# Pairs of up projection tiles in parts 1 to 3 computed as seven block products of quarter sums

## The chip, the cores and the metric

The kernel runs on one core of a Trainium2 chip. The metric is the device time of one execution in microseconds (us). The profile is that of one execution, taken by the hardware profiler.

## The reference, cut to what matters

One inference step of a streaming encoder with two layers (`DEPTH = 2`). 512 prompt rows and 8 x 16 sample rows make 640 rows of 1024 features in float32. Each layer has two kinds of attention and then a feed-forward, which is all that the change touches:

```python
def finish_layer(x, a, b, ga, gb, w_a, w_b, w_o, g1, b1, w_up, w_down, g2, b2):
    mix = (ga * (a @ w_a) + gb * (b @ w_b)) @ w_o
    x = layer_norm(ALPHA * x + mix, g1, b1)
    h = jnp.square(jax.nn.relu(x @ w_up)) @ w_down      # w_up 1024 x 4096, w_down 4096 x 1024
    return layer_norm(ALPHA * x + h, g2, b2)
```

## The kernel before

**Numbers in two halves.** Every float32 operand of a product is split: ScalarE writes a rounded high half (type float32r), and VectorE the low half, value minus high. A product of two operands is three matmuls: high x high, high x low, low x high. `high` and `low` do this for a chunk of weights (128 partitions x 1024), `x_high` and `x_low` for the input, held transposed as `xt_hi` and `xt_lo`, 8 blocks of 128 features by 640 rows.

**The weights** are one stream of chunks of 512 KB. SP loads them in order into four slots of `raw`; the load of a chunk waits (`w_ready`) until the low half of the chunk four places before is made, which frees its slot. Two working slots `s` = 0 and 1 (`w_hi`, `w_lo`) are used in turn. Chunks are counted in pairs: `n` is the pair, `nth` gives it for a place in the stream. Some slots more (`LAST_ROWS`, `NEXT`) lie in the region `r_b`.

**The feed-forward** is cut into four parts of 1024 hidden features (`FF_PARTS`). A part has 8 up tiles (four pairs `u`, `s` = 0 and 1) and then two row groups of down products. `feature_tile` computes one up tile, 128 hidden features by 640 rows: two halves of 320 rows (`HALF`), each a bank of PSUM, 8 blocks `k` and three matmuls in each. Tile `s` uses the banks 4 + 2s and 5 + 2s (`pair(s)`). ScalarE takes the tile out by a ReLU into `tmp1`, makes the high half of the weights of the next pair, VectorE squares into `tmp2`, makes the low half of those weights, ScalarE copies the square's high half, and VectorE writes its low half. The hidden features go to `act_b` in parts 0 and 2 and to `act_a` in parts 1 and 3. `row_group` is a half of the down product: for each `k` and each of five row tiles `r`, three matmuls of 512 columns, into the banks 0, 1, 2, 3 and 7 (`ROW_BANKS`). VectorE adds each finished bank into `rows` (`take`).

**Order.** Each engine runs its own list in order and waits on semaphores (`wait_ge`), written out by hand. `chunk_half_done[s]` and `chunk_done[s]` count the halves of a chunk's matmuls that TensorE has finished, `w_ready[s]` the low halves of weights, `h_ready` the hidden tiles, `relu_done[s]` the tiles taken out of PSUM, `row_evacuated[r]` the row banks taken. Both engines handle the weights of the next pair while TensorE works on this one:

```python
for u in range(0, KT // 2):
    for s in range(2):
        t = l * 32 + part * 8 + 2 * u + s
        act.wait_ge(chunk_done[s], nth(l, AT_FF) + part * 8 + u + 1)
        act.wait_ge(sq_done, t)
        fn(halves(tmp1[:]), pair(s), ACT.Relu).then_inc(relu_done[s], 1)
        high(s, nth(l, AT_FF, 1) + part * 8 + u)
        wait_apart(act, sq_done, t + 1)
        fn(hidden[0][:, 2 * u + s, :], tmp2[:], ACT.Copy).then_inc(h_hi_ready, 1)
```

Of the kernel before, what the change touches and what calls it, by code (L numbers as in the profile page):

```python
# [18 lines left out]
F32 = mybir.dt.float32  # L19
# [20 lines left out]
HALF = ROWS // 2  # L40
BANK = 512
FF_PARTS = 4
ALPHA = (2 * DEPTH) ** 0.25
EPS = 1e-5
QK_SCALE = DH ** -0.5
# [41 lines left out]
def build(nc, x_rows, k_cache, v_cache, swa_kc, swa_vc, swa_k_keep, swa_v_keep, weights, cols,  # L87
# [3 lines left out]
    with ctx:  # L91
# [36 lines left out]
        for hi_at, lo_at in ((0, 4096), (20480, 24576), (8192, 28672), (12288, 16384), (32768, 36864)):  # L128
            n = len(w_hi)
            w_hi.append(at([r_b[0] + hi_at, r_b[1]], f"w_hi{n}", [D], F32R))  # L130
            w_lo.append(at([r_b[0] + lo_at, r_b[1]], f"w_lo{n}", [D], F32R))
        LAST_ROWS, NEXT = (2, 3, 0, 4), (5, 6)

        cos = at(r_keep, "cos", [ROWS], F32)
# [49 lines left out]
        d_rs = at(rb, "d_rs", [P], F32)  # L184
        rb = list(r_b)
        act_b = [at(rb, "act_b_hi", [KT, ROWS], F32R), at(rb, "act_b_lo", [KT, ROWS], F32R)]

        rm = list(r_mix)
        u_p = [at(rm, f"u_p{p}", [2, BANK], F32) for p in range(2)]
# [6 lines left out]
        rm = list(r_mix)  # L196
        ln_g = at(rm, "ln_g", [D], F32)
        ln_b = at(rm, "ln_b", [D], F32)
        rr = list(r_rows)
        s_p = at(rr, "s_p", [8, P], F32)  # L200
        s_pt = at(rr, "s_pt", [8, P], F32)
# [28 lines left out]

        def halves(t):
            return t.rearrange("p (a n) -> p a n", a=2)


        raw_loaded = [sem(f"raw_loaded{j}") for j in range(RAW_SLOTS)]
# [58 lines left out]
        input_rows, out_stored = sem("input_rows"), sem("out_stored")  # L294
        relu_done = [sem(f"relu_done{s}") for s in range(2)]
        sq_done, h_hi_ready, h_ready = sem("sq_done"), sem("h_hi_ready"), sem("h_ready")
        y_stored, keep_stored = sem("y_stored"), sem("keep_stored")
        newton = sem("newton")
        waits_passed = sem("waits_passed")
# [49 lines left out]
        def transposed_tile(r):  # L349

            bank = (4, 0, 2, 0, 2)[r]
            return PS[:, bank:bank + 2, :].rearrange("p a (k n) -> p (a k) n", n=P)

        def norm_tile(l, which, r):
            return (2 * l + which) * RT + r
# [70 lines left out]
        def _(pe):  # L426
            mm = nc.tensor.matmul

            def feature_tile(s, n, hi, lo, which, part=None, between=None, slot=None, order=None):
# [5 lines left out]
                for half, k in order:  # L435
# [8 lines left out]
                    if k == KT - 1:  # L444
                        last.then_inc((chunk_half_done if half == 0 else chunk_done)[s], 1)

            def row_group(n, group, hi, lo, before_k=None, between=None, before_bank=None, banks=ROW_BANKS):

                if between is not None:
# [5 lines left out]
                for k, r in steps:  # L455
                    s, k2 = (k // 2) % 2, k % 2
                    if r == 0:
                        if k2 == 0:
                            pe.wait_ge(w_ready[s], n + (k // 4 + 1))
                        if before_k:  # L460
                            before_k(k)
                    slot = LAST_ROWS[k // 2] if between is not None else s
                    if between and (r, k) in between:
                        between[r, k]()
                    wh = w_hi[slot][:, k2 * BANK:(k2 + 1) * BANK]
                    wl = w_lo[slot][:, k2 * BANK:(k2 + 1) * BANK]
                    if k == 0:

                        pe.wait_ge(row_evacuated[r], group)
                        if r == RT - 1 and before_bank:  # L470
                            before_bank()
# [317 lines left out]
            for l in range(DEPTH):  # L789
# [2 lines left out]

                for v in range(0, 2):
                    row_group(nth(l, AT_V) + 2 * v, l * GROUPS + v, xt_hi, xt_lo,
                              before_bank=lambda: rope_pair_free(l * ROPES + 1), banks=V_BANKS)

                all_heads(pe, l, head)
                last_head_end(l)
# [80 lines left out]
                for v in range(2):  # L879
# [4 lines left out]
                              before_bank=lambda: pe.wait_ge(branch_taken, l * 16 + 16))  # L884

                for part in range(FF_PARTS):
                    hidden = act_b if part % 2 == 0 else act_a
                    if part == 0:

                        first_tiles(l, 1, nth(l, AT_FF))  # L890
                    for u in range(1 if part == 0 else 0, KT // 2):
                        for s in range(2):

                            pe.wait_ge(relu_done[s], l * 16 + 4 * part + u)
                            if s == 1:

                                pe.wait_ge(row_evacuated[RT - 1], l * GROUPS + 4 + 2 * part)
                            feature_tile(s, nth(l, AT_FF) + 8 * part + u, xt_hi, xt_lo, s)
                    def down(v, between=None):
                        row_group(nth(l, AT_FF) + 8 * part + 4 + 2 * v, l * GROUPS + 4 + 2 * part + v,  # L900
                                  hidden[0], hidden[1],
                                  lambda k: pe.wait_ge(h_ready, l * 32 + 8 * part + k + 1), between,

                                  lambda: pe.wait_ge(relu_done[1], l * 16 + 4 * part + 4))

                    if part < FF_PARTS - 1:
                        for v in range(0, 2):
# [7 lines left out]
        def _(act):  # L915
# [310 lines left out]
            def normalise(l, which):  # L1226
# [13 lines left out]
                if more:  # L1240
                    x_high(*at_x, 3)
                    x_high(*at_x, 4)

            eps = col[:, C_EPS:C_EPS + 1]
            act.preload_act_table_set("natural_log_exp_and_others")
            high(0, 0, NEXT[0])
# [8 lines left out]
            for l in range(DEPTH):  # L1255
# [65 lines left out]
                last_groups_high(nth(l, AT_O), True)  # L1321
                normalise(l, 0)

                act.wait_ge(ln_rows, RT * (l + 1))
                load_norm(l, 1)
                for part in range(FF_PARTS):
                    hidden = act_b if part % 2 == 0 else act_a
                    for u in range(0, KT // 2):
                        for s in range(2):
                            t = l * 32 + part * 8 + 2 * u + s  # L1330
                            act.wait_ge(chunk_done[s], nth(l, AT_FF) + part * 8 + u + 1)
                            act.wait_ge(sq_done, t)
                            fn(halves(tmp1[:]), pair(s), ACT.Relu).then_inc(relu_done[s], 1)  # L1333
                            high(s, nth(l, AT_FF, 1) + part * 8 + u)
                            wait_apart(act, sq_done, t + 1)
                            fn(hidden[0][:, 2 * u + s, :], tmp2[:], ACT.Copy).then_inc(h_hi_ready, 1)

                    down = nth(l, AT_FF, 4) + part * 8
                    if part < FF_PARTS - 1:
                        group_high(down)  # L1340
                        for i in (3, 4):
                            for s in range(2):
                                high(s, down + i)
# [11 lines left out]
        def _(dve):  # L1355
# [377 lines left out]
            def half_rows(h):  # L1733
                return lambda r: rows[:, r, bass.ts(h, BANK)]


            v.memset(mask_cols[:], 0.0).then_inc(masks_ready, 1)
            low(0, 0, NEXT[0])
# [31 lines left out]
            for l in range(DEPTH):  # L1770
# [41 lines left out]
                wait_apart(dve, x_rows_loaded, 16 * (l + 1))  # L1812
                take_last_but_one(l * GROUPS + 2, nth(l, AT_O), ALPHA, True)
                take_and_normalise(l, 0, l * GROUPS + 3, nth(l, AT_O) + 2, ALPHA)
                for part in range(FF_PARTS):
                    hidden = act_b if part % 2 == 0 else act_a
                    for u in range(0, KT // 2):
                        for s in range(2):
                            t = l * 32 + part * 8 + 2 * u + s
                            dve.wait_ge(relu_done[s], l * 16 + part * 4 + u + 1)  # L1820
                            dve.wait_ge(h_ready, t)
                            v.tensor_tensor(tmp2[:], tmp1[:], tmp1[:], ALU.mult).then_inc(sq_done, 1)  # L1822
                            low(s, nth(l, AT_FF, 1) + part * 8 + u)
                            dve.wait_ge(h_hi_ready, t + 1)
                            v.tensor_tensor(hidden[1][:, 2 * u + s, :], tmp2[:],
                                            hidden[0][:, 2 * u + s, :].bitcast(F32), ALU.subtract)\
                                .then_inc(h_ready, 1)


                    wait_apart(dve, ln_rows, RT * (l + 1))  # L1830
                    group, n = l * GROUPS + 4 + 2 * part, nth(l, AT_FF) + 8 * part + 4
                    if part < FF_PARTS - 1:
                        for half in range(0, 2):
                            take_group(group + half, n + 2 + 2 * half, half, ALPHA if part == 0 else 1.0)
# [157 lines left out]
```

## Time and profile before

| | |
|---|---|
| Runs | 2302.49, 2303.79, 2306.5 us; median 2303.79 |
| The profiled execution: its own time, its span | 2303.64 us, 2301.8 us |
| TensorE busy | 2257.1 us, 98% of the span |
| VectorE busy | 1129.2 us, 49% |
| ScalarE busy | 914.0 us, 40% |
| Mean granted clock of TensorE | 0.996 of full speed |
| DMA | 107 GB/s over the span |

The span is from the first to the last instruction; a run's own time holds a little around it. Engines are named PE (TensorE matmul), PEld (TensorE weight load), DVE (VectorE), ACT (ScalarE), SP (SyncE, which issues the weight loads). L441 is line 441 of the kernel. Lines of helpers stand for all that they record: L441 to L443 are the matmuls of every feature tile, L474 to L476 those of every row group, L926 every high half of weights, L1396 every low half. Matmuls are pipelined, so each is shown longer than the step from one to the next.

### The profile page before, as it was taken

The numbers are of one execution on the slowest core, as the hardware profiler recorded it, in microseconds if no ns is written. First come the engines' busy times: TensorE is split into PE (matmuls) and PEld (weight loads), VectorE is DVE, ScalarE is ACT, GpSimd is POOL, SyncE is SP. The second block draws the span as 40 slices with busy tenths as digits, with TensorE's granted clock in tenths as the row PEclk, the third lists the DMA queues.
The fourth block names the chain that finished last, engine by engine and source line by source line (L and its number), as shares of the span: only waits on it lengthen the run. The fifth ranks groups of instructions, "written<-read, shape, count | busy, mean of one in ns | idle before, by whom it ended". The sixth has DMA issues, their size and how long they took to land.

```text
span 2301.8 us, 37714 instructions
## 1 busy us (share of the span) xinstructions
PE 2257.1 (98%) x15798; PEld 2061.5 (90%) x15802; DVE 1129.2 (49%) x1853; ACT 914.0 (40%) x1874; POOL 0.2 (0%) x4
## 2 busy tenths in 40 slices
PE   8999999999999999999999999999999999999998
PEld 7888889999989898989888888899999898989897
DVE  3477752375356333324645777423743652423336
ACT  3376651485223222213224666415842232313131
POOL 0000000000000000000000000000000000000000
PEclk9999999999999999999999999999999999999999
DMA  6465532212231222222244555222132322222221
GB/s 231 167 221 190 188 101 70 77 47 84 95 125 55 83 74 74 75 81 74 92 174 181 194 195 195 66 74 67 49 111 74 110 74 74 74 83 74 75 77 69
DMA packets 57479, 247.16 MB, mean 107 GB/s; under 512 B 9912, under 2 KB 10808, under 8 KB 52928
## 3 DMA queue, kind: packets, MB, share of 16 engines
q1 hardware_dynamic: 42128, 153.01, 20.1%
q10 hardware_dynamic: 15184, 91.75, 11.0%
q8 instruction: 126, 2.06, 0.4%
q14 instruction: 41, 0.34, 0.0%
HBM read 228.49 MB, written 18.09 MB: 107 GB/s over the span
## 4 chain that ended last, share of the span: by engine, by line
PE 92%; DVE 4%; ACT 2%; issue 1%; DMA 0%; SPq 0%; DVEq 0%; ACTq 0%
PE PS L441 17%; PE PS L442 17%; PE PS L443 17%; PE PS L474 9%; PE PS L475 9%; PE PS L476 9%; PE PS L601 2%; PE PS L565 1%; PE PS L516 1%; PE PS L728 1%; PE PS L547 1%; PE PS L709 1%; PE PS L615 1%; PE PS L764 1%; DVE small L1440 1%
## 5 line engine op out<-in xcount | busy, mean ns | idle before, releaser
L441 PE MATMUL PS<-xt_hi,w_hi 128*128 128x320 f32 x2368 | 747.8, 316 | 16.6 <-DVE xt_lo L1640 6.4
L443 PE MATMUL PS<-xt_hi,w_lo 128*128 128x320 f32 x2368 | 733.5, 310 | 0.0
L442 PE MATMUL PS<-xt_lo,w_hi 128*128 128x320 f32 x2368 | 733.3, 310 | 0.0
L1396 DVE TENSOR_TENSOR w_lo<-w_raw,w_hi 128x1024 fp32r<-128x1024 f32 x276 | 335.7, 1222 | 448.7 <-ACT w_hi L926 439.5
L926 ACT ACTIVATE w_hi<-w_raw 128x1024 fp32r<-128x1024 f32 x276 | 289.8, 1057 | 577.7 <-PE PS L476 405.0
L441 PEld LDWEIGHTS PS<-xt_hi,w_hi 128*128 128x128 f32 x2368 | 446.5, 189 | 21.0 <-issue 10.4
L442 PEld LDWEIGHTS PS<-xt_lo,w_hi 128*128 128x128 f32 x2368 | 446.8, 189 | 0.4
L443 PEld LDWEIGHTS PS<-xt_hi,w_lo 128*128 128x128 f32 x2368 | 446.2, 188 | 0.0
L474 PE MATMUL PS<-w_hi,act_a_hi 128*128 128x512 f32 x480 | 187.7, 391 | 0.0
L476 PE MATMUL PS<-w_hi,act_a_lo 128*128 128x512 f32 x480 | 186.9, 389 | 0.0
L475 PE MATMUL PS<-w_lo,act_a_hi 128*128 128x512 f32 x480 | 186.8, 389 | 0.0
L1822 DVE TENSOR_TENSOR rope_s<-rope_c 128x640 f32<-128x640 f32 x64 | 52.8, 825 | 266.1 <-ACT rope_c L1333 266.1
L953 ACT ACTIVATE rope_s<-PS 32x320 f32<-32x320 f32 x352 | 150.6, 428 | 40.6 <-DVE z_all L1387 19.3
L1333 ACT ACTIVATE rope_c<-PS 128x640 f32<-128x640 f32 x64 | 45.1, 705 | 297.4 <-PE PS L443 297.4
L441 PE MATMUL PS<-act_b_hi,w_hi 128*128 128x320 f32 x512 | 158.9, 310 | 3.2 <-DVE act_b_lo L1493 3.2
L442 PE MATMUL PS<-act_b_lo,w_hi 128*128 128x320 f32 x512 | 158.2, 309 | 0.0
L443 PE MATMUL PS<-act_b_hi,w_lo 128*128 128x320 f32 x512 | 158.2, 309 | 0.0
L475 PE MATMUL PS<-w_lo,act_b_hi 128*128 128x512 f32 x320 | 124.5, 389 | 0.0
L474 PE MATMUL PS<-w_hi,act_b_hi 128*128 128x512 f32 x320 | 124.5, 389 | 0.0
L476 PE MATMUL PS<-w_hi,act_b_lo 128*128 128x512 f32 x320 | 124.5, 389 | 0.0
L476 PEld LDWEIGHTS PS<-w_hi,act_a_lo 128*128 128x128 f32 x480 | 90.1, 188 | 18.9
L474 PEld LDWEIGHTS PS<-w_hi,act_a_hi 128*128 128x128 f32 x480 | 90.1, 188 | 18.6 <-issue 0.5
(188 smaller groups left out, 2782.3 us busy)
## 6 DMA issues: line engine op xcount, KB each, us to landing
w_raw<-in_weights SPq DMA_DIRECT2D x276, 512.0 KB, 3.5
kc<-in_k_cache ACTq DMA_DIRECT2D x16, 2048.0 KB, 8.1
vc<-in_v_cache ACTq DMA_DIRECT2D x16, 2048.0 KB, 8.3
v_out<-rows ACTq DMA_DIRECT2D x2, 2560.0 KB, 8.8
k_out<-k_t ACTq DMA_DIRECT2D x16, 320.0 KB, 2.4
rows<-in_x_rows SPq DMA_DIRECT2D x5, 512.0 KB, 7.8
rows<-in_x_rows ACTq DMA_DIRECT2D x1, 2560.0 KB, 10.6
x_all<-rows ACTq DMA_DIRECT2D x1, 2560.0 KB, 8.8
```

Of the source, the lines that this page charges most:

```text
L441: mm(out, wh, hi[:, k, c], start=(k == 0), stop=False)
L442: mm(out, wh, lo[:, k, c], start=False, stop=False)
L443: last = mm(out, wl, hi[:, k, c], start=False, stop=(k == KT - 1))
L474: mm(out, xh, wh, start=(k == 0), stop=False)
L475: mm(out, xh, wl, start=False, stop=False)
L476: last = mm(out, xl, wh, start=False, stop=(k == KT - 1))
L601: last = mm(PS[:, bank, first:first + w], q_t[p][d, i * P:(i + 1) * P], k_t[p][d, 0:w], start=False, stop=True, skip_group_check=True)
L926: fn(w_hi[slot][:], raw[:, j, :], ACT.Copy).then_inc(w_hi_made[s], 1)
L953: last = fn(rope_s[dst:dst + 32, half * HALF:(half + 1) * HALF], PS[src:src + 32, bank_of(0, half), 0:HALF], ACT.Copy, scale=scale)
L1333: fn(halves(tmp1[:]), pair(s), ACT.Relu).then_inc(relu_done[s], 1)
L1396: v.tensor_tensor(w_lo[slot][:], raw[:, raw_of(s, n)[0], :], w_hi[slot][:].bitcast(F32), ALU.subtract)\
L1822: v.tensor_tensor(tmp2[:], tmp1[:], tmp1[:], ALU.mult).then_inc(sq_done, 1)
```

## The change

Two up tiles (256 hidden features) of parts 1 to 3 are now one product of a 2 x 2 block matrix with a 2 x 2 block matrix, by Winograd's form of Strassen's scheme: seven block products in place of eight. The weights' quarters A11, A12 (first tile, feature blocks 0 to 3 and 4 to 7) and A21, A22 (second tile) meet the input's quarters B11, B12 (blocks 0 to 3, rows 0 to 319 and 320 to 639) and B21, B22 (blocks 4 to 7).

- **Input sums** t1 = B12 - B11, t2 = B22 - t1, t3 = B22 - B12, t4 = B21 - t2 are made once a layer, in part 0, by VectorE (`x_sums`, `x_sum_low`) and ScalarE (`t_high`), 1280 elements a partition each.
- **Weight sums**, of 512 elements: S1 = A21 + A22, A11 - A21, S2 = S1 - A11, A12 - S2 (`weight_sums`). The factors of the seven products are, in order `o` = 0 to 6: A11, S1, S2, A12, A11 - A21, A12 - S2, A22; the sums overwrite the quarters in `raw`, all but S1, which has a buffer; each factor is split by `part_highs` and `part_low`. Factors 0 to 3 have buffers of their own in `r_mix`, 4 lies in slot 0, 5 and 6 in slot 1.
- **Sums in PSUM.** Product 0 goes to bank X1 = 4 and product 1 to X4 = 6. ScalarE copies X1 to X2 = 3 (`up_seed` 0), and product 2 adds to it without a start flag; product 3 adds to X1, which is then the first tile's first half. X2 is copied to X3 = 7 (seed 1), product 4 adds to X2, product 5 to X3; X2 is copied to X5 = 5 (seed 2), and product 6 adds to it. ScalarE copies X4 to `p5` in SBUF (`up_fifth`), and VectorE adds it to X2 and X3 (`up_add`) to give the second halves of the two tiles.
- **Out of PSUM.** ReLU is four instructions of 320 elements, and the square is done twice on ScalarE, once into the high half (`up_square_high`) and once in float32 in place (`up_square`), of which VectorE subtracts the high half (`up_low`).
- **One activation buffer**, `act_a`, for all parts. `r_b` holds the input sums. `load_norm(l, 1)` moves from the start of the feed-forward to part 3. In parts 0 to 2 the weight sums and halves of the next part's first pair are made during the second down group.

Cut diff, TensorE (semaphores of the new kernel: `part_ready` counts low halves of factors 0 to 4, `seeded` the copies between banks, `up_taken` the sums taken by `up_add`, `c11_taken` and `c21_taken` the first ReLU halves):

```diff
+            def combined_pair(q, n):
+                b11, b21, b22 = [(quarter(xt_hi, k, r), quarter(xt_lo, k, r)) for k, r in ((0, 0), (1, 0), (1, 1))]
+                def product(x, o, moving, first):
+                    for k in range(KH):
+                        wh, wl = part_hi[o][:, k * P:(k + 1) * P], part_lo[o][:, k * P:(k + 1) * P]
+                        mm(up_bank(x), wh, moving[0][:, k], start=first and k == 0, stop=False, skip_group_check=True)
+                        mm(up_bank(x), wh, moving[1][:, k], start=False, stop=False, skip_group_check=True)
+                        last = mm(up_bank(x), wl, moving[0][:, k], start=False, stop=(k == KH - 1),
+                                  skip_group_check=True)
+                    return last
+                pe.wait_ge(part_ready, 5 * q + 1)
+                pe.wait_ge(c11_taken, q)
+                product(X1, 0, b11, True).then_inc(up_done, 1)
+                pe.wait_ge(part_ready, 5 * q + 2)
+                pe.wait_ge(p5_copied, q)
+                product(X4, 1, (t_hi[1], t_lo[1]), True).then_inc(up_done, 1)
+                pe.wait_ge(part_ready, 5 * q + 3)
+                pe.wait_ge(seeded, 3 * q + 1)
+                product(X2, 2, (t_hi[2], t_lo[2]), False).then_inc(up_done, 1)
+                pe.wait_ge(part_ready, 5 * q + 4)
+                product(X1, 3, b21, False).then_inc(chunk_half_done[0], 1)
+                pe.wait_ge(part_ready, 5 * q + 5)
+                pe.wait_ge(seeded, 3 * q + 2)
+                product(X2, 4, (t_hi[3], t_lo[3]), False).then_inc(chunk_done[0], 1)
+                pe.wait_ge(w_ready[0], n + 1)
+                product(X3, 5, b22, False).then_inc(chunk_half_done[1], 1)
+                pe.wait_ge(w_ready[1], n + 1)
+                pe.wait_ge(seeded, 3 * q + 3)
+                product(X5, 6, (t_hi[4], t_lo[4]), False).then_inc(chunk_done[1], 1)
...
+                            combined_pair(*pair_at(l, part, u))
```

ScalarE and VectorE, in each the list for one pair (the pieces are as told above; `part_highs(..., u + 1, ...)` and `part_low(..., u + 1, ...)` work for the next pair):

```diff
+            def combined_pair(l, part, u):
+                last = u == FF_PAIRS - 1
+                down = nth(l, AT_FF, 4) + part * 8
+                if u > 0:
+                    up_square(l, part, u - 1, 0)
+                    up_relu(l, part, u - 1, 1, 0)
+                    part_highs(l, part, u, (6,))
+                up_seed(l, part, u, 0)
+                if u > 0:
+                    up_square_high(l, part, u - 1, 1)
+                if not last:
+                    part_highs(l, part, u + 1, (0,))
+                if u > 0:
+                    up_square(l, part, u - 1, 1)
+                up_fifth(l, part, u)
+                if not last:
+                    part_highs(l, part, u + 1, (1,))
+                up_seed(l, part, u, 1)
+                if not last:
+                    part_highs(l, part, u + 1, (2,))
+                up_relu(l, part, u, 0, 0)
+                if not last:
+                    part_highs(l, part, u + 1, (3,))
+                up_seed(l, part, u, 2)
+                up_relu(l, part, u, 1, 1)
+                if not last:
+                    part_highs(l, part, u + 1, (4, 5))
+                else:
+                    high(0, down)
+                up_relu(l, part, u, 0, 1)
+                up_square_high(l, part, u, 0)
+                if last:
+                    up_square(l, part, u, 0)
+                    up_relu(l, part, u, 1, 0)
+                    high(1, down)
+                    up_square_high(l, part, u, 1)
+                    up_square(l, part, u, 1)
...
+            def combined_pair(l, part, u):
+                last = u == FF_PAIRS - 1
+                down = nth(l, AT_FF, 4) + part * 8
+                if not last:
+                    weight_sums(l, part, u + 1, 1)
+                    weight_sums(l, part, u + 1, 3)
+                if u > 0:
+                    up_low(l, part, u - 1, 0)
+                    part_low(l, part, u, 6)
+                    up_low(l, part, u - 1, 1)
+                if not last:
+                    part_low(l, part, u + 1, 0)
+                    weight_sums(l, part, u + 1, 2)
+                    for o in (1, 2, 3):
+                        part_low(l, part, u + 1, o)
+                up_add(l, part, u, 1)
+                if not last:
+                    weight_sums(l, part, u + 1, 4)
+                    part_low(l, part, u + 1, 4)
+                else:
+                    low(0, down)
+                up_add(l, part, u, 0)
+                if not last:
+                    part_low(l, part, u + 1, 5)
+                else:
+                    up_low(l, part, u, 0)
+                    low(1, down)
+                    up_low(l, part, u, 1)
```

`up_add` of the second tile (odd, bank X2) waits for `p5_copied`, product 4 and seed 2; that of the first (even, bank X3) for product 5. A second ReLU half waits for its `up_add`.

## Rows read from the trace of the kernel before

**Rows 1.** The page: busy time by engine, and the chain that ended last:

```profile
PE 2257.1 (98%) x15798; PEld 2061.5 (90%) x15802; DVE 1129.2 (49%) x1853; ACT 914.0 (40%) x1874; POOL 0.2 (0%) x4
...
PE 92%; DVE 4%; ACT 2%; issue 1%; DMA 0%; SPq 0%; DVEq 0%; ACTq 0%
```

**Rows 2.** Windows: from:to and length in us, busy us (count), clock, DMA:

```profile
core 0: us, PE busy (x) PEld busy (x) DVE busy (x) ACT busy (x) POOL busy (x), PEclk, DMA share, GB/s
10.00:15.00 5.00, 2.77 (x14) 2.46 (x12) 3.65 (x4) 2.99 (x3) 0.00 (x0) 1.00 1.03 392
15.00:20.00 5.00, 4.81 (x24) 4.83 (x25) 1.22 (x2) 0.00 (x0) 0.00 (x0) 0.66 1.04 405
938.20:994.50 56.30, 56.30 (x370) 55.11 (x369) 22.29 (x24) 19.14 (x24) 0.00 (x0) 1.00 0.22 75
994.50:1048.90 54.40, 54.40 (x258) 46.21 (x257) 16.61 (x18) 8.48 (x8) 0.00 (x0) 1.00 0.23 78
```

**Rows 3.** The timeline of ScalarE: start us, length us, instruction, idle before:

```profile
938.55 0.70 ACT L1333 ACTIVATE rope_c<-PS 128x640 f32<-128x640 f32 x1 [5.92 <-PE PS L443]
939.15 1.05 ACT L926 ACTIVATE w_hi<-w_raw 128x1024 fp32r<-128x1024 f32 x1
...
945.59 0.70 ACT L1333 ACTIVATE rope_c<-PS 128x640 f32<-128x640 f32 x1 [4.62 <-PE PS L443]
...
1119.05 1.06 ACT L926 ACTIVATE w_hi<-w_raw 128x1024 fp32r<-128x1024 f32 x1 [4.79 <-PE PS L476]
...
1295.29 1.75 ACT L953 ACTIVATE rope_s<-PS 32x320 f32<-32x320 f32 x4
```

**Rows 4.** The timeline of TensorE where one up tile ends and the next begins:

```profile
938.20 0.31 PE L443 MATMUL PS<-xt_hi,w_lo 128*128 128x320 f32 x1
938.35 0.31 PE L441 MATMUL PS<-xt_hi,w_hi 128*128 128x320 f32 x1
```

**Rows 5.** ScalarE's groups by line and form: count, busy us, mean ns of one, idle before:

```profile
L926 ACT ACTIVATE w_hi<-w_raw 128x1024 fp32r<-128x1024 f32 x276 | 289.8, 1057 | 577.7 <-PE PS L476 405.0 <-PE PS L443 166.6 <-DMA w_raw<-in_weights 5.8
L953 ACT ACTIVATE rope_s<-PS 32x320 f32<-32x320 f32 x352 | 150.6, 428 | 40.6 <-DVE z_all L1387 19.3 <-PE PS L443 16.2
...
L1333 ACT ACTIVATE rope_c<-PS 128x640 f32<-128x640 f32 x64 | 45.1, 705 | 297.4 <-PE PS L443 297.4
...
L1010 ACT ACTIVATE d_p<-PS,small 128x640 f32<-128x640 f32 x32 | 25.1, 790 | 22.0 <-DVE small L1506 22.0
L1336 ACT ACTIVATE act_b_hi<-rope_s 128x640 fp32r<-128x640 f32 x32 | 23.7, 741 | 0.9
...
L1159 ACT ACTIVATE s_pt<-PS 128x512 f32<-128x512 f32 x40 | 21.8, 595 | 39.1 <-PE PS L709 39.1
```

**Rows 6.** The timeline of VectorE:

```profile
939.28 0.82 DVE L1822 TENSOR_TENSOR rope_s<-rope_c 128x640 f32<-128x640 f32 x1 [5.39 <-ACT rope_c L1333]
...
1120.14 4.63 DVE L1396 TENSOR_TENSOR w_lo<-w_raw,w_hi 128x1024 fp32r<-128x1024 f32 x4 [4.44 <-ACT w_hi L926]
...
1136.72 0.69 DVE L1652 SCALAR_TENSOR_TENSOR rows<-rows,PS 128x512 f32<-128x512 f32 x1 [0.27 <-PE PS L476]
1137.55 0.69 DVE L1657 BATCH_NORM_STATS2 ln_st<-rows 128x6 f32<-128x512 f32 x1
```

**Rows 7.** VectorE's groups by line and form:

```profile
L1379 DVE SCALAR_TENSOR_TENSOR rope_c<-PS,cos 128x320 f32<-128x320 f32 x88 | 42.9, 488 | 41.8 <-ACT rope_s L953 41.1 <-issue 0.3
...
L1825 DVE TENSOR_TENSOR act_b_lo<-rope_s,act_b_hi 128x640 fp32r<-128x640 f32 x32 | 26.2, 818 | 0.0
...
L1387 DVE TENSOR_TENSOR q_t<-rope_c,rope_s 128x512 f32<-128x512 f32 x16 | 11.1, 692 | 1.7
```

**Rows 8.** The timeline of VectorE, then of TensorE, where TensorE waits for VectorE:

```profile
1164.70 1.22 DVE L1640 TENSOR_TENSOR xt_lo<-PS,xt_hi 128x1024 fp32r<-128x1024 f32 x1 [1.95 <-ACT xt_hi L970]
...
1166.07 0.38 PE L441 MATMUL PS<-xt_hi,w_hi 128*128 128x320 f32 x1 [1.59 <-DVE xt_lo L1640]
1166.30 0.31 PE L442 MATMUL PS<-xt_lo,w_hi 128*128 128x320 f32 x1
```

More of the change, by code:

```diff
@@ L42 @@
 FF_PARTS = 4
+FF_PAIRS = KT // 2
+KH = KT // 2
 ALPHA = (2 * DEPTH) ** 0.25
@@ L198, in build @@
         ln_b = at(rm, "ln_b", [D], F32)
+        rm = list(r_mix)
+        s_one = at(rm, "s_one", [BANK], F32)
+        p5 = at(rm, "p5", [HALF], F32)
+        rm[0] = r_mix[0] + 4096
+        part_hi, part_lo = [None] * 7, [None] * 7
+        for o in (3, 0, 1, 2):
+            part_hi[o] = at(rm, f"part_hi{o}", [BANK], F32R)
+            part_lo[o] = at(rm, f"part_lo{o}", [BANK], F32R)
+        for o, slot, cols_of in ((4, 0, slice(0, BANK)), (5, 1, slice(0, BANK)), (6, 1, slice(BANK, D))):
+            part_hi[o], part_lo[o] = w_hi[slot][:, cols_of], w_lo[slot][:, cols_of]
         rr = list(r_rows)
@@ L882, in _ @@
                               three_transposes(l, 1) if v else None,
-                              before_bank=lambda: pe.wait_ge(branch_taken, l * 16 + 16))
-                for part in range(FF_PARTS):
[L887 to L898, printed above, removed]
+                              before_bank=lambda r: r == RT - 1 and pe.wait_ge(branch_taken, l * 16 + 16))
@@ new lines, in up_fifth, with up_relu @@
+            def up_fifth(l, part, u):
+                q, n = pair_at(l, part, u)
+                act.wait_ge(up_done, 3 * q + 2)
+                if q:
+                    act.wait_ge(up_taken, 2 * q)
+                fn(p5[:], up_bank(X4), ACT.Copy).then_inc(p5_copied, 1)
+            def up_relu(l, part, u, odd, half):
+                q, n = pair_at(l, part, u)
+                tile = (tmp2 if odd else tmp1)[:, half * HALF:(half + 1) * HALF]
+                if half == 1:
+                    act.wait_ge(up_taken, 2 * q + (1 if odd else 2))
+                    fn(tile, tile, ACT.Relu).then_inc(relu_odd if odd else relu_even, 1)
+                elif odd:
+                    act.wait_ge(chunk_done[1], n + 1)
+                    fn(tile, up_bank(X5), ACT.Relu).then_inc(c21_taken, 1)
+                else:
+                    act.wait_ge(chunk_half_done[0], n + 1)
+                    act.wait_ge(h_ready, l * 32 + 8 * part + max(0, 2 * u - 1))
+                    fn(tile, up_bank(X1), ACT.Relu).then_inc(c11_taken, 1)
@@ L1322, in _ @@
                 normalise(l, 0)
-                act.wait_ge(ln_rows, RT * (l + 1))
-                load_norm(l, 1)
-                for part in range(FF_PARTS):
[L1327 to L1336, printed above, removed]
+                for u in range(FF_PAIRS):
+                    for s in range(2):
+                        t = l * 8 + 2 * u + s
+                        act.wait_ge(chunk_done[s], nth(l, AT_FF) + u + 1)
+                        act.wait_ge(sq_done, t)
+                        fn(halves(tmp1[:]), pair(s), ACT.Relu).then_inc(relu_done[s], 1)
+                        high(s, nth(l, AT_FF, 1) + u)
+                        wait_apart(act, sq_done, t + 1)
+                        fn(act_a[0][:, 2 * u + s, :], tmp2[:], ACT.Copy).then_inc(h_hi_ready, 1)
+                    for t in ((), (1,), (2, 3), (4,))[u]:
+                        t_high(l, t)
@@ L1338, in _ @@
+                for part in range(FF_PARTS):
                     down = nth(l, AT_FF, 4) + part * 8
+                    if part > 0:
+                        part_highs(l, part, 0, range(7))
+                        for u in range(FF_PAIRS):
+                            combined_pair(l, part, u)
                     if part < FF_PARTS - 1:
                         group_high(down)
-                        for i in (3, 4):
-                            for s in range(2):
-                                high(s, down + i)
-                    else:
+                        for s in range(2):
+                            high(s, down + 3)
+                    else:
+                        q, n = pair_at(l, part, FF_PAIRS - 1)
+                        act.wait_ge(part_ready, 5 * (q + 1))
+                        act.wait_ge(s_summed, 4 * (q + 1))
+                        load_norm(l, 1)
@@ new lines, in x_sum_low, with weight_sums @@
+            def x_sum_low(l, t):
+                dve.wait_ge(t_hi_ready, 4 * l + t)
+                dve.wait_ge(t_ready, 4 * l + min(t + 2, 4))
+                v.tensor_tensor(t_lo[t][:], t_full[t][:], t_hi[t][:].bitcast(F32), ALU.subtract)\
+                    .then_inc(t_lo_ready, 1)
+            def weight_sums(l, part, u, which):
+                q, n = pair_at(l, part, u)
+                first, second = raw[:, raw_of(0, n)[0], :], raw[:, raw_of(1, n)[0], :]
+                a11, a12, a21, a22 = first[:, 0:BANK], first[:, BANK:D], second[:, 0:BANK], second[:, BANK:D]
+                if which == 1:
+                    for s in range(2):
+                        j, loads = raw_of(s, n)
+                        dve.wait_ge(raw_loaded[j], 16 * loads)
+                    if q:
+                        dve.wait_ge(s_summed, 4 * q - 1)
+                        dve.wait_ge(part_ready, 5 * q - 3)
+                    v.tensor_tensor(s_one[:], a21, a22, ALU.add).then_inc(s_summed, 1)
+                elif which == 3:
+                    dve.wait_ge(s_summed, 4 * q + 1)
+                    v.tensor_tensor(a21, a11, a21, ALU.subtract).then_inc(s_summed, 1)
+                elif which == 2:
+                    dve.wait_ge(s_summed, 4 * q + 2)
+                    dve.wait_ge(part_ready, 5 * q + 1)
+                    v.tensor_tensor(a11, s_one[:], a11, ALU.subtract).then_inc(s_summed, 1)
+                elif which == 4:
+                    dve.wait_ge(s_summed, 4 * q + 3)
+                    dve.wait_ge(part_ready, 5 * q + 4)
+                    v.tensor_tensor(a12, a12, a11, ALU.subtract).then_inc(s_summed, 1)
```

213 lines of the change are left out of this document (188 added, 25 removed).

## The prediction

> **What bounds the kernel now.** I read the page first. In its busy line and its chain [rows 1] the reader is to see that TensorE is busy for 98% of the span and makes up 92% of the chain that ended last. So a matmul taken away counts, as long as nothing that replaces it makes TensorE wait. Then the windows [rows 2]: in the feed-forward's up stretch (938.2 to 994.5 us) TensorE is busy all the time at full clock, while VectorE is busy 22.3 of 56.3 us and ScalarE 19.1. Those two have room, and the change spends it. Next the matmul's pitch: ScalarE starts on a finished tile at 938.55 and on the next at 945.59 [rows 3], 7.04 us for 48 matmuls, so 146.7 ns each (their shown 0.31 us overlap). The TensorE timeline [rows 4] runs through the switch of tile, bank and weights at 938.20 to 938.35 with the same step, though each tile is preceded by three waits: a wait that is already met costs nothing. Last come the durations and hand-offs of the other two engines [rows 5 to 8].
>
> **What the change removes.** A pair of up tiles is 2 x 2 x 8 x 3 = 96 matmuls of 320 columns, 14.08 us. Seven products of 4 x 3 matmuls make 84, 12.32 us, or 1.76 us a product. Parts 1 to 3 of two layers hold 24 pairs: 24 x 12 = 288 matmuls fewer, 288 x 0.1467 = 42.2 us. The down products and part 0 keep theirs. The Trainium skill, TensorE: Matmul & The Clock Gate, section "Wait — 56ns, not 53.3ns?", puts the pitch at columns over 2.4 GHz plus about 2.5 ns, which is 135.8 ns here; by it the saving would be 39.1 us, an estimate. The trace has 146.7.
>
> **What ScalarE and VectorE now do in a pair.** ScalarE: seven `part_highs` of 512 elements at 0.63 (the 0.595 of a 512 copy from PSUM plus the 0.035 by which the 640 form from SBUF, 0.740, exceeds that from PSUM, 0.705) [rows 5]; three seeds, `up_fifth` and two ReLU halves of 320 from PSUM at 0.44 (0.705 less 320 x 0.83 ns, the slope between the 640 and 1024 forms, 0.740 and 1.057; the 32-partition copy of 320 takes 0.428); two ReLU halves from SBUF at 0.47; four squares of 640 at 0.74. Together 10.95 us, and as neighbours without a dependency overlap by 0.10 (four 1.057 us in 3.90) [rows 3], some 9.1 us. VectorE: eleven operations of 512 at 0.69, two of 320 at 0.49, two of 640 at 0.82, 10.2 us, 8.8 with its overlap of 0.09 (four in 4.63) [rows 6, 7]. Both lie under 12.32, so neither is the bound by amount. By order they may be.
>
> **The loop that is nearly closed.** Seed 0 (X1 to X2) must land before product 2 of the same pair, and on ScalarE it stands behind a chain that starts with the end of product 4 of the pair before. A hand-off between engines costs 0.03 us, 0.20 of tail after TensorE's last slot (938.20 + 0.147 to 938.55) [rows 3, 4, 6]. From product 4's end: seed 2, 0.20 + 0.03 + 0.44 = 0.67; odd `up_add` 0.52, 1.19; odd ReLU half 0.50, 1.69; `part_highs` 4, 0.53, 2.22; its low 0.72, 2.94; even `up_add` 0.39, 3.33; even ReLU half 0.50, 3.83; even square-high 0.77, 4.60; even square 0.77, 5.37; odd first ReLU half 0.34, 5.71; `part_highs` 6, 0.53, 6.24; seed 0, 0.34, 6.58; TensorE's start 0.15 behind its releaser (1164.70 + 1.22 to 1166.07) [rows 8], 6.73. TensorE meanwhile runs products 5, 6, 0 and 1: 4 x 1.76 = 7.04. The slack is 0.31 us, the thinnest in the pair. Seed 1 has about 0.9, seed 2 about 1.1, and the weights' halves are ready 6 us or more ahead. I cost the steady pair at no stall.
>
> **Where a stall does come: from the last pair to the down products.** Before, the down tile's weights were made a tile ahead. Now `high(0, down)` stands behind the odd ReLU half at 1.69 after product 4's end, and every down product stands behind its low part on TensorE: high 0.96, 2.65; low 0.03 + 1.22, 3.90; start 0.15 and the slower first step (0.23 instead of 0.147) [rows 8] make 4.13. Products 5 and 6 cover 3.52. So 0.61 us, six times: 3.7 us. The second slot's low part ends 8.9 us after product 4 and is wanted at 10.9, thirty matmuls later (54.4 / 240 = 0.2267 us each [rows 2]): hidden. The other border is hidden too: at a part's start products 0 to 4 have their halves from the down stretch; 5 and 6 get theirs 2.1 us in and are wanted at 8.8 and 10.6.
>
> **Part 0.** Twelve new VectorE operations of 1280 elements, 1.22 + 256 x 1.04 ns = 1.49 each, and four such copies on ScalarE, 17.9 and 5.1 us a layer, lie in the gaps of the part's second to fourth pair, where VectorE is used to 40% [rows 2]. Laid out in order, the last six end 11.0 us after part 0's last tile, the low part of the next down weights at 12.2, wanted at 13.6. The cover is 1.4 us; without it the price is what is over, twice. The single activation buffer costs nothing: it is written again only behind product 3 of the next part, when TensorE has left the down products. `load_norm`'s two loads move from the start of the feed-forward to the last part, 50 us before their use, behind waits met long before; the weight loads queued on SP start when a pair's products 5 and 6 have their low halves, 8 us ahead of need.
>
> **Sum.** 2303.64 (the profiled execution; the runs' median is 2303.79) - 42.2 + 3.7 = 2265.1; I say 2265 us.
>
> **Bounds of what no row shows.** An activation that writes PSUM: below, nothing at all, which only widens the slack; above, the slowest 640 form, 0.79 [rows 5], 0.35 more. I take 0.44, the same form into SBUF. Two seeds lie in the loop, 0.70 - 0.31 = 0.39 a pair for the 18 pairs with one before them, 7 us, and one in each border, 2.1: 2274. Overlap between neighbours that carry several waits: rows show 0.10 behind two met waits (939.15 begins before 938.55 + 0.70) [rows 3], and none for four copies in a row (1.75 for four of 0.428) [rows 3]. Without it ScalarE is never free; both streams laid out in program order with these durations then make TensorE wait up to 0.9 us a pair, 6.1 a layer: 2265 + 12 = 2277. Both ends together come to about 2286. A better end than 2261.4 would need matmuls that cost less than now; only the border stall can vanish.
>
> **Rivals.**
> *Seeds late (0.22).* The loop above is longer than 7.04. For it: 0.31 us of slack over twelve steps, none of the four kinds of 320 and 512 measured in this place. Against: every step is a plain form with a row near it. 2270 to 2286, say 2276.
> *Each product starts like a released one (0.05).* Seven starts a pair, each with an open wait, at 0.15 + 0.08: 7 x 24 x 0.23 = 38.6, which with the border eats the gain: 2304, no change. Against: a tile's start costs nothing now [rows 4], and most of the new waits are met early. This is the case in which the change does not do what it is for.
> *ScalarE's order becomes the bound, and the kernel is slower (0.08).* One mechanism: hand-offs behind two to four waits cost more than 0.03. The only dearer one seen is 0.14, after a wait with a semaphore step of its own (1136.72 + 0.69 to 1137.55) [rows 6]. The loop has twelve steps, so past 0.03 of extra each TensorE waits; the pair loses its 1.76 us from (1.76 + 0.31) / 12 = 0.17 extra each. At 0.22 extra the loop gives 2.33 x 18 = 42, the six borders 5 x 0.22 = 1.1 each, 6.6: 2314 us. Were it 0.11 extra, 18 + 3: 2286.
> *The clock.* At 15 to 20 us the granted clock was 0.66 on average, between its two levels of 1.2 and 2.4 GHz, after a stretch with TensorE busy for 2.8 of 5 us [rows 2]. At the lower level the 24 pairs would take twice 12.32, 296 us more. Against: the largest wait here is under a microsecond. The Trainium skill, TensorE: Matmul & The Clock Gate, "A second HAM failure mode: psum-queue depth-cycling", tells of such a fall where TensorE idles briefly between groups in changing banks; that is this product's shape. I give it 0.01.
>
> **How the numbers follow.** Forecast 0.61, its own range 2262 to 2270; seeds late 0.22; between 2286 and 2299 0.03; no change 0.05; slower 0.08; the clock 0.01. Range 2261 to 2286 takes the first two. Within 0.2% (4.6 us) is about what cannot be told from no change. Faster 0.61 + 0.22 + 0.03 = 0.86, same 0.05, slower 0.09.
>
> **What would show it.** 288 matmuls of 320 columns fewer; up stretches of parts 1 to 3 near 49.3 us instead of 56.3, full clock. TensorE's waits: six of about 0.6 us on `w_lo` at a down product's first matmul; under 0.1 us on a seed before product 2. A wait on a seed in 18 pairs shows the late seeds; ScalarE without gaps shows its order; waits at part 0's third down tile show the sums. Most likely to prove me wrong is the loop's slack of 0.31 us.

## The result and the profile after

The changed kernel takes 2267.3 us (2263.23 to 2268.48, 4 runs) beside 2304.61 us (2302.49 to 2306.5, 4 runs) of the kernel before: ratio 0.9835, 95% interval 0.9818 to 0.9852. It is faster by 1.6%, and 2265 us was forecast. The profiled execution took 2268.48 us, its span 2266.7.

The page, its span, its busy line and its chain, beside [rows 1]:

```profile
span 2266.7 us, 38089 instructions
...
PE 2219.7 (98%) x15514; PEld 2021.7 (89%) x15514; DVE 1262.6 (56%) x2093; ACT 1041.9 (46%) x2194; POOL 0.2 (0%) x4
...
PE 91%; DVE 4%; ACT 3%; issue 2%; DMA 0%; SPq 0%; DVEq 0%; ACTq 0%
```

TensorE is still the bound, with 37.4 us less of busy time; VectorE has 133 us more and ScalarE 128. The windows of [rows 2] lie about 6.9 us behind the stretches themselves: each takes in the end of one stretch and the start of the next. From first matmul to first matmul the same two stretches of the kernel before are:

```profile
core 0: us, PE busy (x) PEld busy (x) DVE busy (x) ACT busy (x) POOL busy (x), PEclk, DMA share, GB/s
931.31:987.63 56.32, 56.32 (x386) 56.31 (x384) 21.62 (x24) 17.81 (x22) 0.00 (x0) 1.00 0.23 75
987.63:1042.05 54.42, 54.42 (x242) 45.05 (x241) 17.29 (x19) 9.81 (x10) 0.00 (x0) 1.00 0.24 78
```

The lengths differ from those of [rows 2] (56.30 and 54.40) by 0.02 us, so what is reckoned from them holds; in the up stretch VectorE was busy for 21.6 us and ScalarE for 17.8, not 22.3 and 19.1. In the changed kernel the windows of an up stretch with block products, of the down stretch behind it, and of an up stretch in the second layer are:

```profile
core 0: us, PE busy (x) PEld busy (x) DVE busy (x) ACT busy (x) POOL busy (x), PEclk, DMA share, GB/s
821.74:871.57 49.83, 49.44 (x337) 49.17 (x335) 33.05 (x52) 33.46 (x66) 0.00 (x0) 1.00 0.26 85
871.57:926.12 54.55, 54.55 (x240) 45.17 (x241) 22.28 (x28) 13.89 (x18) 0.00 (x0) 1.00 0.24 78
1944.49:1994.53 50.04, 49.64 (x337) 49.16 (x335) 33.04 (x52) 33.47 (x66) 0.00 (x0) 1.00 0.26 85
```

An up stretch now has 4 x 84 = 336 matmuls (384 before; a window also counts those that are still running at its edges). Without any stall it would be 336 x 0.1467 = 49.28 us. The three of the first layer take 49.83, 49.84 and 49.83, those of the second 50.04, 50.04 and 50.07: 0.55 and 0.77 over, and each down stretch behind them 0.12 over 54.43. So the six parts save 42.2 - 3 x (0.55 + 0.12) - 3 x (0.77 + 0.12) = 37.5 us. The two profiles' own times lie 35.2 apart; the other 2.4 us lie outside the feed-forwards, where the kernels are the same, and I don't assign them. Those parts differ by that much and more from one execution to another. Between the layers alone, from the end of the first layer's last up stretch to the start of part 1's in the second layer it is 864.2 us here, 862.8 in the kernel before, and 860.0 to 864.3 in the experiments below. The medians lie 37.3 apart.

Where the 0.55 goes is seen at the border, where the last up product of a part ends and the first down product begins. The timeline of TensorE there:

```profile
870.87 0.31 PE L504 MATMUL PS<-t_hi,w_lo 128*128 128x320 f32 x1
871.57 0.50 PE L561 MATMUL PS<-w_hi,act_a_hi 128*128 128x512 f32 x1 [0.40 <-DVE w_lo L1615]
871.91 0.40 PE L562 MATMUL PS<-w_lo,act_a_hi 128*128 128x512 f32 x1
872.14 0.40 PE L563 MATMUL PS<-w_hi,act_a_lo 128*128 128x512 f32 x1
```

The step (from one matmul's start to the next one's) from 870.87 to 871.57 is 0.70 us where 0.147 would do, and the first down step is 0.34 in place of 0.23: 0.67 us in all. The idle of 0.40 in brackets is less than that, since the drawn lengths overlap: read the starts. TensorE's list of waits names the same stall in all six parts (us in total, times, longest us), and lists none on a seed:

```profile
PE PS L561 <- DVE w_lo L1615: 2.4, 6, 0.4
```

What TensorE waits for there, the timelines of ScalarE and of VectorE:

```profile
868.84 0.47 ACT L1399 ACTIVATE rope_s<-rope_s 128x320 f32<-128x320 f32 x1 [0.72 <-DVE rope_s L2035]
869.22 1.04 ACT L1024 ACTIVATE w_hi<-w_raw 128x1024 fp32r<-128x1024 f32 x1
```

```profile
870.29 1.22 DVE L1615 TENSOR_TENSOR w_lo<-w_raw,w_hi 128x1024 fp32r<-128x1024 f32 x1 [1.49 <-ACT w_hi L1024]
```

The high half of the down weights starts behind the odd ReLU half (L1399), the low half 0.03 us after the high half's end, and TensorE 0.06 after the low half's end.

**The loop** of a steady pair. ScalarE's timeline from seed 2 (855.38) to the next pair's seed 0 (861.43):

```profile
855.38 0.42 ACT L1384 ACTIVATE PS<-PS 128x320 f32<-128x320 f32 x1 [0.28 <-PE PS L504]
856.52 0.47 ACT L1399 ACTIVATE rope_s<-rope_s 128x320 f32<-128x320 f32 x1 [0.72 <-DVE rope_s L2035]
856.90 1.14 ACT L1368 ACTIVATE w_hi<-w_raw 128x512 fp32r<-128x512 f32 x2
858.67 0.47 ACT L1399 ACTIVATE rope_c<-rope_c 128x320 f32<-128x320 f32 x1 [0.63 <-DVE rope_c L2035]
859.18 0.74 ACT L1412 ACTIVATE act_a_hi<-rope_c 128x640 fp32r<-128x640 f32 x1
859.95 0.74 ACT L1417 ACTIVATE rope_c<-rope_c 128x640 f32<-128x640 f32 x1
860.59 0.42 ACT L1402 ACTIVATE rope_s<-PS 128x320 f32<-128x320 f32 x1
860.91 0.62 ACT L1368 ACTIVATE w_hi<-w_raw 128x512 fp32r<-128x512 f32 x1
861.43 0.43 ACT L1384 ACTIVATE PS<-PS 128x320 f32<-128x320 f32 x1
```

VectorE's `up_add` between seed 2 and the odd ReLU half:

```profile
856.00 0.49 DVE L2035 TENSOR_TENSOR rope_s<-PS,p 128x320 f32<-128x320 f32 x1 [0.17 <-ACT PS L1384]
```

And TensorE at the end of product 4, and at the start of product 2 of the next pair:

```profile
855.03 0.31 PE L504 MATMUL PS<-t_hi,w_lo 128*128 128x320 f32 x1
855.18 0.31 PE L502 MATMUL PS<-xt_hi,w_hi 128*128 128x320 f32 x1
...
862.07 0.31 PE L504 MATMUL PS<-t_hi,part_lo 128*128 128x320 f32 x1
862.22 0.31 PE L502 MATMUL PS<-t_hi,part_hi 128*128 128x320 f32 x1
```

Ends counted from product 4's end at 855.18, as laid out in the prediction and as measured:

| step | laid out | measured |
|---|---|---|
| seed 2 | 0.67 | 0.62 |
| odd `up_add` | 1.19 | 1.31 |
| odd ReLU half | 1.69 | 1.81 |
| even ReLU half | 3.83 | 3.96 |
| even square-high, square | 4.60, 5.37 | 4.74, 5.51 |
| odd first ReLU half | 5.71 | 5.83 |
| `part_highs` 6 | 6.24 | 6.35 |
| seed 0 | 6.58 | 6.68 |
| with TensorE's start | 6.73 | 6.83 |
| product 2 wants it | 7.04 | 7.04 |

The seed is there 0.21 us early. One step differs by more than 0.05, the hand-off from seed 2 to `up_add`: 0.20 us in place of 0.03. The groups behind the durations, by form (count, busy us, mean ns of one, idle before):

```profile
L1368 ACT ACTIVATE part_hi<-w_raw 128x512 fp32r<-128x512 f32 x72 | 44.3, 623 | 22.3 <-DVE w_raw L2009 22.3
L1384 ACT ACTIVATE PS<-PS 128x320 f32<-128x320 f32 x72 | 30.6, 425 | 27.1 <-PE PS L504 26.9
L2021 DVE TENSOR_TENSOR part_lo<-w_raw,part_hi 128x512 fp32r<-128x512 f32 x72 | 49.1, 689 | 15.5 <-ACT part_hi L1368 13.6
L1973 DVE TENSOR_TENSOR t<-b,t 128x1280 f32<-128x1280 f32 x2 | 3.0, 1492 | 0.1
```

### The profile page after: what moved, and what is told of

Same layout as the page of the kernel before. It is cut to its first block, busy times and chain, and to the rows that moved or that the text cites. A ratio compares the mean times of both kernels' runs of the same rounds, so it can differ in the third digit from the quotient of the medians.

```text
span 2266.7 us, 38089 instructions
## 1 busy us (share of the span) xinstructions
PE 2219.7 (98%) x15514; PEld 2021.7 (89%) x15514; DVE 1262.6 (56%) x2093; ACT 1041.9 (46%) x2194; POOL 0.2 (0%) x4
## 4 chain that ended last, share of the span: by engine, by line
PE 91%; DVE 4%; ACT 3%; issue 2%; DMA 0%; SPq 0%; DVEq 0%; ACTq 0%
PE PS L489 13%; PE PS L490 12%; PE PS L491 12%; PE PS L561 10%; PE PS L563 10%; PE PS L562 10%; PE PS L502 4%; PE PS L504 4%; PE PS L503 4%; PE PS L688 2%; PE PS L652 1%; PE PS L603 1%; PE PS L815 1%; PE PS L634 1%; PE PS L851 1%
## 5 line engine op out<-in xcount | busy, mean ns | idle before, releaser
L489 PE MATMUL PS<-xt_hi,w_hi 128*128 128x320 f32 x1600 | 511.9, 320 | 16.7 <-DVE xt_lo L1859 6.4
L491 PE MATMUL PS<-xt_hi,w_lo 128*128 128x320 f32 x1600 | 497.3, 311 | 0.0
L490 PE MATMUL PS<-xt_lo,w_hi 128*128 128x320 f32 x1600 | 497.2, 311 | 0.0
L489 PEld LDWEIGHTS PS<-xt_hi,w_hi 128*128 128x128 f32 x1600 | 303.4, 190 | 20.9 <-issue 10.4
L561 PE MATMUL PS<-w_hi,act_a_hi 128*128 128x512 f32 x800 | 313.0, 391 | 2.4 <-DVE w_lo L1615 2.4
L563 PE MATMUL PS<-w_hi,act_a_lo 128*128 128x512 f32 x800 | 311.6, 390 | 0.0
L562 PE MATMUL PS<-w_lo,act_a_hi 128*128 128x512 f32 x800 | 311.5, 389 | 0.0
L490 PEld LDWEIGHTS PS<-xt_lo,w_hi 128*128 128x128 f32 x1600 | 303.7, 190 | 0.2
L491 PEld LDWEIGHTS PS<-xt_hi,w_lo 128*128 128x128 f32 x1600 | 302.9, 189 | 0.0
L562 PEld LDWEIGHTS PS<-w_lo,act_a_hi 128*128 128x128 f32 x800 | 150.3, 188 | 30.4
```

Of the source, the lines that this page charges most:

```text
L489: mm(out, wh, hi[:, k, c], start=(k == 0), stop=False)
L490: mm(out, wh, lo[:, k, c], start=False, stop=False)
L491: last = mm(out, wl, hi[:, k, c], start=False, stop=(k == KT - 1))
```

## The experiments

The questions were whether the 0.67 us at the border and the second layer's 0.22 are all that the changed kernel loses, whether the loop is as near to its limit as laid out, and whether the moves around the products cost anything.

**The changed kernel again.** No edit; it stands on the same chip as the next three.

> The changed kernel once more, as the mark for the next three. All theories: about 37 us under the kernel before (2267), six waits of 0.4 us for the low half of the down weights at the end of parts 1 to 3.

2265.52 us (2261.78 to 2268.79, 4 runs) beside 2302.09: ratio 0.9837 (0.9823 to 0.9852), the same six waits of 0.4 us at the borders, span 2267.0. The result repeats.

**Both places cleared.** The first down weights of parts 1 to 3 go to a third slot and are made a step earlier, and seed 0 is issued ahead of the copy that stands before it:

```diff
 # ScalarE (TensorE reads slot NEXT[0] for the first two k of the first down group)
-                    part_highs(l, part, u, (6,))
                 up_seed(l, part, u, 0)
                 if u > 0:
+                    part_highs(l, part, u, (6,))
...
                 if not last:
                     part_highs(l, part, u + 1, (2,))
+                else:
+                    high(0, down, NEXT[0])
...
                     part_highs(l, part, u + 1, (4, 5))
-                else:
-                    high(0, down)
...
 # VectorE
+                else:
+                    low(0, down, NEXT[0])
                 up_add(l, part, u, 1)
                 if not last:
                     weight_sums(l, part, u + 1, 4)
                     part_low(l, part, u + 1, 4)
-                else:
-                    low(0, down)
```

> Two moves in the changed kernel: the down product's first weights are made in a spare slot before the last pair's odd ReLU half, and seed 0 stands ahead of the seventh factor's high half. My theory (TensorE is the bound, 0.67 us lost at each of six borders, plus now and then a late seed 0): no wait at the borders, 4.1 us less, with the rare late seeds 4.4 us less, so 2263 against 2267. Rival (the missing 3 to 5 us come from the products themselves, whose starts cost more than before): the borders close and the time moves by under 1 us.

2262.24 us (2260.26 to 2264.61, 4 runs), ratio 0.9824 (0.9809 to 0.9839): 3.3 us under the changed kernel by medians, whose runs overlap with these. The stretches say it more sharply than times or spans, which also hold what varies outside the feed-forwards: the six parts take 4.7 us less, and no wait on `w_lo` is left. The windows of the same two stretches:

```profile
823.66:872.93 49.27, 49.27 (x337) 49.27 (x336) 33.48 (x52) 34.37 (x68) 0.00 (x0) 1.00 0.29 97
872.93:927.36 54.43, 54.43 (x243) 45.05 (x242) 21.94 (x27) 12.98 (x17) 0.00 (x0) 1.00 0.21 68
```

49.27 to 49.28 in all six parts is the matmuls' own 49.28: TensorE no longer stops in them. This is the fastest of all the kernels timed over several runs. Its product starts also answer the rival in which each start costs something, in TensorE's timeline:

```profile
869.26 0.31 PE L504 MATMUL PS<-t_hi,w_lo 128*128 128x320 f32 x1
869.41 0.31 PE L502 MATMUL PS<-xt_hi,w_hi 128*128 128x320 f32 x1
```

A product begins with other weights, another bank and waits of its own, here already met, and the step is 0.15 us.

**The border alone.** The edit above without the move of seed 0.

> Only the first of the two moves of e2_both: the first down weights in a spare slot, made early. My theory: the six border waits vanish, 4.0 us less than the changed kernel (2263 by its own time), and rare late seeds before product 2 stay possible. Rival: the wait reappears at the second slot's weights, which are made after product 6, so less than 1 us is gained.

One run, 2260.78 us; a single time can't be set against the medians within 2 us, but the stretches can be read: 49.27 to 49.28 in the first layer, 49.49 to 49.51 in the second. So the border move takes away 0.67 a part in both layers, and the second layer's 0.22 a part (0.77 less 0.55) is another thing, which goes with the seed's move. It sits in one pair of each second-layer part, in the changed kernel at 1954, 2071 and 2188 us. The timeline of VectorE shows the second of them:

```profile
2071.37 0.49 DVE L2035 TENSOR_TENSOR rope_s<-PS,p 128x320 f32<-128x320 f32 x1 [0.52 <-ACT PS L1384]
```

`up_add` starts 0.56 us behind the end of seed 2 where 0.20 is usual, and that 0.35 more is over the slack of 0.21 by 0.14. Product 2, in the timeline of TensorE, then starts late:

```profile
2077.09 0.31 PE L504 MATMUL PS<-t_hi,part_lo 128*128 128x320 f32 x1
2077.37 0.38 PE L502 MATMUL PS<-t_hi,part_hi 128*128 128x320 f32 x1
2077.60 0.30 PE L503 MATMUL PS<-t_lo,part_hi 128*128 128x320 f32 x1
```

It is 0.13 late, and the next step is 0.08 longer (0.23). With both places cleared the same three hand-offs are as late (0.55 to 0.57) and the stretches are still 49.28: the earlier seed covers them.

**Three more copies in the loop.** Three further copies of 320 elements from bank to bank, whose results are not used, before seed 0 in the 18 pairs that have one before them:

```diff
                     up_square(l, part, u - 1, 0)
+                    act.wait_ge(chunk_done[1], pair_at(l, part, u - 1)[1] + 1)
+                    act.wait_ge(spare_done, 3 * (l * 9 + (part - 1) * 3 + u - 1))
+                    for i in range(3):
+                        act.wait_ge(row_evacuated[i], l * GROUPS + 4 + 2 * part)
+                        fn(PS[:, i, 0:HALF], up_bank(X5), ACT.Copy).then_inc(spare_done, 1)
                     up_relu(l, part, u - 1, 1, 0)
```

> Three copies of 320 elements from bank to bank more on ScalarE ahead of seed 0, in the 18 pairs with one before them; nothing else changes. My theory (a loop from product 4 over VectorE and ScalarE to the next product 2, with 0.21 us to spare): 3 x 0.34 - 0.21 = 0.81 us a pair, 14.6 us in all, so 2282, and TensorE waits for a seed before product 2 in each of the 18 pairs. Rival (ScalarE has room by amount, 9.1 us busy of 12.32, so what is added disappears in its gaps): within 1 us of the changed kernel, 2267.

2280.56 us (2278.12 to 2282.36, 4 runs), ratio 0.9904 (0.9887 to 0.992): 15.0 us above the changed kernel on the same chip; the six up stretches are 15.9 longer than in the changed kernel's first profile. TensorE's waits:

```profile
PE PS L503 <- ACT PS L1385: 12.4, 18, 1.0
```

And its timeline at such a product 2:

```profile
849.83 0.31 PE L505 MATMUL PS<-t_hi,part_lo 128*128 128x320 f32 x1
850.77 0.38 PE L503 MATMUL PS<-t_hi,part_hi 128*128 128x320 f32 x1 [0.63 <-ACT PS L1385]
850.99 0.30 PE L504 MATMUL PS<-t_lo,part_hi 128*128 128x320 f32 x1
```

The step is 0.94 where 0.147 would do: 0.79 late, and the next step is 0.08 longer. ScalarE's three copies took 1.07 us as a group and pushed the rest by 0.99; 0.99 - 0.79 = 0.20 is the slack, the 0.21 of the table by another way. In three pairs, those of the second layer whose `up_add` is late, the step is 1.3.

**One more copy.** The same with one copy instead of three.

> The same with one copy more. My theory: 0.34 - 0.21 = 0.13 us a pair, 2.3 us in all, and 18 short waits before product 2. Rival of room by amount: no wait at all.

One run, 2268.45 us, which can't be told from the changed kernel by time. In the trace product 2 starts 0.13 to 0.14 us late in 15 of the 18 pairs, so one copy of 0.36 is over the slack, which bounds it from above; 0.36 - 0.13 = 0.23. This wait stands in no list; only the steps show it:

```profile
951.74 0.31 PE L505 MATMUL PS<-t_hi,part_lo 128*128 128x320 f32 x1
952.02 0.38 PE L503 MATMUL PS<-t_hi,part_hi 128*128 128x320 f32 x1
952.24 0.31 PE L504 MATMUL PS<-t_lo,part_hi 128*128 128x320 f32 x1
```

The other three pairs, again those with the late `up_add`, start 0.5 late.

From one border to the next the parts are 105.02 us in the first layer beside 104.37, so 0.22 a pair; in both layers it sums to about 4.3 us, not the 2.3 expected. The expectation had left out the slower step behind each late start and the three pairs that come 0.5 late.

**The old tiles with the moves around them.** The kernel before, with the single activation buffer, a working slot moved out of `r_b`, and the input sums of part 0, which nothing uses here; no block product. `load_norm` stays where it was. The core of it:

```diff
-                    hidden = act_b if part % 2 == 0 else act_a
+                    hidden = act_a
...
+                        if part == 0:
+                            x_sums(l, u)
+                    if part == 0:
+                        x_sum_low(l, 4)
```

> The kernel before with all of the change but the block products: one activation buffer, the moved slot, and the input sums t1 to t4 made (and not used) in part 0 by VectorE and ScalarE. The output is whole. My theory: all of it lies beside the matmuls, so 2304, within 1 us of the kernel before. Rival (the sums delay part 0's last weights, or the single buffer makes the first tile of a part wait for the down products): up to 2 us a layer at the third down tile of part 0, or 0.8 us at each part, 4 to 6 us more, 2308 to 2310.

2304.72 us (2303.36 to 2307.52, 10 runs) beside 2304.1 (2301.62 to 2308.22, 13 runs): ratio 1.0005 (0.9996 to 1.0015). The sums' twelve VectorE operations and four copies a layer and the one buffer cost nothing that can be measured. VectorE's group of low halves of the sums, and the window of an up stretch, still 56.31:

```profile
L1792 DVE TENSOR_TENSOR t_lo<-t,t_hi 128x1280 fp32r<-128x1280 f32 x8 | 11.6, 1488 | 0.4
...
821.03:877.34 56.31, 56.31 (x385) 56.31 (x384) 21.62 (x24) 17.85 (x22) 0.00 (x0) 1.00 0.23 75
```

## Why the prediction was right

**The matmuls, -42.2 us: right.** With both stalls gone an up stretch is 49.27 us, 7.04 under the 56.31 to 56.32 of the kernel before, and six times that is 42.2. By the Trainium skill, TensorE: Matmul & The Clock Gate, section "Wait — 56ns, not 53.3ns?", it would have been 39.1, an estimate; its pitch is short of these float32r matmuls before and after (135.8 ns beside 146.7), and the measured step decides.

**The borders, +3.7 us: right.** They cost 0.56 for the late start and 0.11 for the slow first step, 0.67 x 6 = 4.0. The place, the count and the instruction waited for were the forecast ones; the 0.17 that `up_add` starts late is partly given back, since the low half released TensorE after 0.06 rather than 0.15 us. Moving that one pair of instructions, alone in the border run, took it away, so the cause is shown.

**The loop, no stall: right, and it is the thinnest place.** The slack is 0.21 us, not 0.31, by the table, by three more copies (0.20) and by one more (0.23). The difference is one hand-off, 0.17 us longer than laid out, of which shorter steps on ScalarE gave back 0.07. Of the 18 pairs, three of the second layer go over the slack, 0.22 us each, 0.7 us in all: a term that the sum lacked, so "no stall in the steady pair" holds for 15 of them. The rival *seeds late* names the right mechanism and needs 0.4 us a pair; three more copies made it real, at 0.87 us in 15 of the pairs and about 1.2 in three.

**Sum.** The stretches give -42.2 + 4.0 + 0.7 = -37.5 where -38.5 was forecast. The profiled execution is 3.4 us above 2265.1: 1.0 of it is this, and 2.4 lie outside the feed-forwards, of which the forecast says nothing.

**Durations no row showed.** The copy from bank to bank took 0.425 (taken: 0.44), `part_highs` 0.623 (0.63), the ReLU half from SBUF 0.47 (0.47), a sum of 1280 elements 1.49 (1.49). Neighbours on ScalarE overlap by 0.10 behind waits too (two of 0.62 in 1.14), so the bound of 2277 without overlap did not come.

**Part 0, nothing: right.** Its last up tile ends at 767.32, the last low half of the sums 11.2 us later (11.0 laid out), and the next down weights at 12.3 (12.2), with 13.6 wanted. The old form with the sums measures 1.0005.

**The other rivals.** *Each product starts like a released one* falls with the 0.15 us steps at product starts. *ScalarE's order* needed 0.17 us more in each of twelve hand-offs; one had it. *The clock* stayed at 1.00, the 2.4 GHz level, in the windows of all six up stretches, with waits of 0.4 us at the borders; even with 18 waits of 0.6 to 1.0 us (three more copies) it was 1.00 in all six. By this, no sign was seen of the fall that the Trainium skill, TensorE: Matmul & The Clock Gate, section "A second HAM failure mode: psum-queue depth-cycling", tells of for short idle times between groups in changing banks.

**Open.** Why one hand-off from seed 2 to `up_add` in each second-layer part takes 0.55 us instead of 0.20. It is not scatter: it is there, 0.55 to 0.57 us long, in all six profiles of kernels with block products, always in the first, the second and the third pair of the layer's parts 1, 2 and 3. In VectorE's records, waits included, the three instructions stand 128 apart in each of the six, and a packet of 8 KB on the instruction queue (q14) starts 0.64 to 0.91 us after each of them. That makes the loading of instructions a suspect. No run moves the place, so it is not shown.

## What to carry to other kernels

When fewer matmuls are bought with more work on the other engines, write out the one dependency loop that closes through them, step by step from rows, and hold it against the matmul time that covers it: here it foretold a slack of 0.31 us in 7.04, and 0.21 was there. Look then at the ends of the loop over tiles, where the pipeline's next item is of another kind: the only regular stall, 0.67 us six times, sat there, and an early slot for one pair of instructions took it away. A slack so thin is worth widening although the sum calls it free: three of the 24 hand-offs from seed 2 to `up_add` took 0.35 us more than the others, in the same places in every profile, and only the kernel with the earlier seed did not pay for them.

## What the runs showed of the hardware that was not expected

- In the changed kernel the hand-off from seed 2 to `up_add` took 0.20 us instead of 0.03 in 21 of the 24 pairs, and 0.55 to 0.57 in the other three. `up_add` carries four waits; that they are the reason was not tested.
- A matmul that is released late costs more than its wait: the step behind a late start is 0.22 to 0.23 us instead of 0.147 (320 columns), and 0.31 to 0.35 instead of 0.227 (512 columns), in the late starts of the feed-forwards and around them.
- Lateness of 0.13 us at a product's start, 15 times over with one more copy, appears in no list of waits. It is seen only in the steps between starts and in the length of a stretch.
- A ScalarE copy of 320 elements from bank to bank took 0.42 to 0.44 us, as long as a ReLU of 320 elements from a bank to SBUF (0.42).
